# Three plain MLP steps ahead of 41 Strassen steps, with the token forms made behind six weight pieces

## The reference, cut to what matters

```python
h2 = rms_norm(x, norm2_g[layer]) * (1 + sc2[:, None]) + sh2[:, None]
ff = (jax.nn.silu(h2 @ w_gate[layer]) * (h2 @ w_up[layer])) @ w_down[layer]
x = x + g2[:, None] * ff
```

## Time and profile before

| | us |
|---|---|
| median of 3 runs | 2255.48 |
| lowest, highest | 2254.44, 2259.04 |
| the profiled execution | 2251.56 |
| its span | 2250.0 |

### The profile page before, as it was taken

How to read it: one execution, slowest core, us unless ns; L and a number is a source line. 1 busy time by engine, 2 the same in 40 slices (tenths; PEclk the granted TensorE clock), 3 DMA queues, 4 the chain that set the end, 5 groups by cost and what they waited for, 6 DMA issues and landing times.

```text
span 2250.0 us, 32144 instructions
## 1 busy us (share of the span) xinstructions
PE 2193.9 (98%) x10856; PEld 1831.2 (81%) x10856; DVE 1614.6 (72%) x2264; ACT 844.9 (38%) x1202; POOL 246.2 (11%) x300
## 2 busy tenths in 40 slices
PE   7999999999999998999999999999999999999996
PEld 4878888777777886888888888888888788888885
DVE  6986777777867898888988888889888522242234
ACT  4224333455453114444444444444444422232221
POOL 4012222000014331000000000000000000011111
PEclk9999999999999999999999999999999999999998
DMA  9895666533525982233333333333333633353333
GB/s 333 296 356 169 206 215 213 176 124 134 201 78 216 334 281 102 98 113 119 124 126 122 119 114 125 117 119 124 126 123 111 225 96 97 97 170 97 97 99 110
DMA packets 134552, 354.40 MB, mean 158 GB/s; under 512 B 21769, under 2 KB 46489, under 8 KB 133985
## 3 DMA queue, kind: packets, MB, share of 16 engines
q1 hardware_dynamic: 124498, 319.08, 42.6%
q0 software_dynamic: 8992, 34.41, 4.2%
q10 hardware_dynamic: 1008, 0.21, 0.0%
HBM read 334.47 MB, written 19.18 MB: 157 GB/s over the span
## 4 chain that ended last, share of the span: by engine, by line
PE 86%; DMA 5%; DVE 4%; POOL 2%; issue 2%; ACT 0%; SPq 0%; DVEq 0%; ACTq 0%; POOLq 0%
PE PS L930 10%; PE P L930 6%; PE PS L934 5%; PE T L983 4%; PE T L982 4%; PE T L981 4%; PE P L622 4%; PE P L624 3%; PE P L623 3%; PE P L934 3%; PE T L930 3%; PE S L930 3%; PE PS L622 3%; PE PS L623 3%; PE PS L624 3%; DMA adar<-in_w_ada 2%
## 5 line engine op out<-in xcount | busy, mean ns | idle before, releaser
L1439 DVE TENSOR_TENSOR W_lo<-raw,W_hi 128x1024 fp32r<-128x1024 f32 (+2 forms) x256 | 283.4, 1107 | 344.4 <-ACT W_hi L1012 343.7
L1012 ACT ACTIVATE W_hi<-raw 128x1024 fp32r<-128x1024 f32 (+2 forms) x256 | 236.8, 926 | 594.9 <-PE T L983 179.5
L1959 DVE TENSOR_TENSOR W_lo<-raw,W_hi 128x1024 fp32r<-128x1024 f32 x160 | 195.5, 1222 | 44.8 <-ACT W_hi L1328 40.7
L1328 ACT ACTIVATE W_hi<-raw 128x1024 fp32r<-128x1024 f32 x160 | 169.5, 1060 | 134.0 <-PE P L934 67.4
L1962 DVE TENSOR_TENSOR raw<-raw 128x1024 f32<-128x1024 f32 x160 | 194.7, 1217 | 0.0
L622 PE MATMUL PS<-H,W_hi 128*128 128x512 f32 x416 | 169.1, 406 | 18.3 <-POOL ident L2187 11.0
L622 PE MATMUL P<-H,W_hi 128*128 128x512 f32 x432 | 177.2, 410 | 4.0 <-DVE H L1915 3.3
L1328 ACT ACTIVATE H<-raw 128x1024 fp32r<-128x1024 f32 x120 | 126.8, 1057 | 133.3 <-DVE raw L1962 72.9
L624 PE MATMUL P<-H,W_lo 128*128 128x512 f32 x432 | 169.8, 393 | 0.0
L623 PE MATMUL P<-H,W_hi 128*128 128x512 f32 x432 | 169.7, 393 | 0.0
L624 PE MATMUL PS<-H,W_lo 128*128 128x512 f32 x416 | 164.0, 394 | 0.0
(11 more groups left out here) (334 smaller groups left out, 4854.7 us busy)
## 6 DMA issues: line engine op xcount, KB each, us to landing
raw<-in_w_gu SPq DMA_DIRECT2D x176, 512.0 KB, 3.3
raw<-in_w_in SPq DMA_DIRECT2D x72, 512.0 KB, 3.5
adar<-in_w_ada SPq DMA_DIRECT2D x72, 512.0 KB, 4.5
att<-in_w_ada SPq DMA_DIRECT2D x32, 1024.0 KB, 10.7
att<-in_w_ada SPq DMA_DIRECT2D x56, 512.0 KB, 5.1
raw<-in_w_down SPq DMA_DIRECT2D x64, 384.0 KB, 3.1
raw<-in_w_down SPq DMA_DIRECT2D x64, 320.0 KB, 2.8
raw<-in_w_out SPq DMA_DIRECT2D x32, 512.0 KB, 5.0
```

The lines of the kernel that those rows point to most:

```text
L1012: act.activation(w_parts(slot)[0][:, 0:cols], raw[:, raw_slot * PW:raw_slot * PW + cols], ACT.Copy).then_inc(hi_done, 1)
L1328: act.activation(form_parts(FORM_SLOT[a])[0], raw_form(FORM_RAW[a]), ACT.Copy).then_inc(hi_done, 1)
L1439: dve.tensor_tensor(lo[:, 0:cols], raw[:, raw_slot * PW:raw_slot * PW + cols], hi[:, 0:cols].bitcast(F32), ALU.subtract).then_inc(lo_done, 1)
L1959: dve.tensor_tensor(lo, raw_form(FORM_RAW[a]), hi.bitcast(F32), ALU.subtract).then_inc(lo_done, 1)
```

## The change

NPL falls from 4 to 3, so step 3 is made as a Strassen step, 41 in all, and all counters that start from NPL move with it. The parts of the T forms now have only two plain steps, 1 and 2, with six pieces: a table T_AT gives the parts behind each, (0), (1, 2), (3, 4), (5), (6), (7). The low parts of part 7 stand in the last plain step behind part 7 (and the low parts of 6). `make_t(u)` has a new wait, for all six instructions of the part before it, since it writes `Ea` and `Eb` again and two parts may now follow each other without a split between them.

```diff
-NPL = 4
+NPL = 3
+T_AT = ((0,), (1, 2), (3, 4), (5,), (6,), (7,))
 FS = FT - NPL
...
             for f in range(1, NPL):
                 for j in range(1, 4):
                     split_gu(f, j)
-                    if 3 * f - 4 + j < HALF:
-                        t_high_half(3 * f - 4 + j)
+                    for u in T_AT[3 * f - 4 + j]:
+                        t_high_half(u)
                 act.wait_ge(used, MLP0 + 4 * f + 2)
...
                 s0 = 6 * u
+                if u:
+                    dve.wait_ge(t_step, s0)
                 half = slice(u * HS, u * HS + HS)
...
             for f in range(1, NPL):
                 for j in range(1, 4):
                     split_gu(f, j)
-                    u = 3 * f - 4 + j
-                    if u < HALF:
+                    for u in T_AT[3 * f - 4 + j]:
                         make_t(u)
-                    if 0 < u <= HALF:
-                        t_low(u - 1)
+                        if u > 0:
+                            t_low(u - 1)
+                if f == NPL - 1:
+                    t_low(HALF - 1)
                 split_gu(f + 1, 0) if f < NPL - 1 else split_form(NPL, "A11")
```

## The result

The changed kernel takes 2264.17 us (median of 5 runs, 2261.30 to 2265.91) against 2255.48 us before (5 runs, 2252.93 to 2259.04): ratio 1.0038, 95% interval 1.0027 to 1.0049. It is slower by 0.38%, 8.6 us, between 6.1 and 11.0.

The account below looks back on a forecast made before the run. The prediction took TensorE, busy 98% of the span, to bound the kernel. It summed -2.20 + 5.67 + 1.6 = +5.1 us onto the median 2255.48, giving 2260.6 us, 0.22% slower, range 2257.0 to 2264.5.

Parts of the forecast that it names:

- The step saved: In the MLP, a plain step of 21.76 us on TensorE becomes a Strassen step of 19.56 us: -2.20 us.
- The chain of splits: Pieces 2 and 3 of step 1: two T parts behind one split delay the next weight pieces on TensorE, +5.67 us.
- Step 2 and the switch: Step 2 and the passage to form A11: one part per piece, split done 1.8 us ahead of need, nothing lost.
- The clock: Behind TensorE's 4.1 us idle: one stretch at 1.2 GHz, +1.6 us, from a price between 0 and 3.2.
- The three rows that I compared: Earlier TensorE pauses bounding the clock price: 2.02 and 2.19 us brought a fall to 1.2 GHz, 2.88 us did not.
- The third rival: TensorE's pauses bring a further slow clock stretch: +1.6 us more, 2262.2 us, or 2263.8 with both; chance 0.19.
- The second rival: ScalarE's and VectorE's queues overlap, hiding the doubled parts: no wait over 2.2 us in sum, 2253.3 with none; chance 0.06.

Follow-up runs that it names:

- the repeat: The changed kernel measured once more with no edit: 2265.20 us against 2255.95 before, ratio 1.0034.
- the evenly placed parts: Changed kernel, parts 0 and 1 behind piece 1, then one behind each split, ScalarE copying weight pieces ahead of T copies: 2254.44 us against 2255.95 before.
- ScalarE's order: Changed kernel, with only ScalarE copying a weight piece ahead of the second part's T copies, VectorE's order kept: 2259.82 us, ratio 1.0022 to before.
- doubled parts alone: Changed kernel with four plain steps again, keeping only the new placing of the T parts and the new wait: 2266.55 us, ratio 1.0042 to before.
- one doubled piece: Changed kernel with four plain steps, only parts 1 and 2 behind one split, all others single: 2257.89 us, ratio 1.0009 to before.
- the one with the busy pause: Changed kernel plus twelve unused matmuls on TensorE ahead of piece 0 of step 2: 2259.89 us, ratio 1.0017 to before.

## Why the prediction was right, point by point

The direction, the two late pieces and what they wait for were forecast as they came. The number is 3.5 us short of the measured 8.6, and it was in part luck that the median fell inside the range, by 0.3 us: the repeat's 2265.20 us lies above it. Here is each term.

**The step saved, -2.20 us: right.** 802.83 - 783.27 = 19.56 us for the added Strassen step, and the evenly placed parts, with no wait left, gave the 2.20 us back in the profile.

**The chain of splits, +5.67 us: right, term by term.** Piece 3 of step 1 was forecast 1.2 us late and is 1.09 late (920.44 - 902.91 against 916.52 - 900.08); the idle of TensorE is 0.93 us where some 1.0 was said. Piece 0 of step 2 was forecast 5.56 us late and is 5.46 late, with 4.08 us of idle for 4.1 forecast. Step 2 and the switch bring no wait, as said. The added wait cost nothing that shows: part 2, which it guards, starts 1.35 us after the low halves ahead of it (913.63 and 914.98 us), where the rows gave 1.34.

**The clock, +1.6 us: the term that was mis-sized.** The mechanism was right, since with TensorE kept busy 2.95 us came back. But behind the pause of 4.08 us the clock stayed at 1.2 GHz not for some 3.4 us as behind the pauses of 2.02 and 2.19 us but for 6.1, and 15 matmuls took 6.41 us for 3.41: with the restart that is 3.03 us in the changed kernel, 2.64 in its repeat, and 1.53 behind the 3.40 us pause of the run with ScalarE's order changed. I took a price from pauses half as long. The three rows that I compared are of one execution, and how long the clock stays down moved the sum, not only the spread. The row nearest to this pause in length, 2.88 us without a fall, spoke for less, and was one outcome of two: the pause at that place brought a fall in 4 of the 8 profiles that left it as it was.

**The sum.** -2.20 us, 5.46 us of lateness and the 3.03 us with restart and clock make +6.3 us, what the stretch shows, and 2261.8 us. The median lies 2.4 us above that. The third rival, more clock than one stretch, gives 2262.2 to 2263.8 us and is nearest. Its mechanism came in part: the first pause brought no fall, the second brought one nearly twice as long, and the pause ahead of the down projection brought one in the profile of the changed kernel and in its repeat. The second rival, waits hidden by overlap of the queues, is excluded for this order, and right for another one: its argument for, that VectorE has the time in steps 1 and 2, is what the even placing used.

**What stays open.** In seven comparisons the difference to before, by the ratio, lies above what the stretch shows, by 0.4 to 2.3 us: +8.6 for +6.3, +7.7 for +5.9, +9.5 for +8.4, +3.8 for +3.5, +5.0 for +3.9, +2.0 for +1.6, -1.6 for -2.2. Each difference is inside its interval, but all have one sign. The granted clock of every run, not only of the profiled ones, points at falls of the clock elsewhere. Its mean is 0.9872 in the changed kernel and in its repeat, and 0.9896 in the 27 runs of before. Counted as (1 - clock) x span, an estimate that takes TensorE as always busy, the changed kernel lost 5.5 us more than before, give or take 2, where the stretch has 3.0 and 2.6. In the same count the other kernels lost more than their stretch shows too, by 1.8 (doubled parts alone), 2.0 (ScalarE's order), 1.4 (one doubled piece) and 1.0 us (evenly placed), and the one with the busy pause 0.4 less. That is the size of what is open, but each figure is uncertain by 1 to 2 us, and no run shows which pauses it is or why they would cost more with the change.

## What to carry to other kernels

When work on one engine has to fit behind pieces that another engine consumes at a fixed pace, sum the work over each piece and not over the stage: here it fitted in total (42.5 of 43.6 us) and still cost 8.4 us where two pieces in a row carried 9.2 us of it against a pace of 5.44 and a lead of 2.86. Put the split that is waited for ahead of work that is not, on each engine that handles it. And count a pause of the matmul engine together with the matmuls behind it: filling four pauses with matmuls whose result is dropped took the kernel with evenly placed parts from 1.6 to 6.5 us below before, more than the 2.2 us that the change had to give. Most of that gain is not the change's: these pauses are in the kernel before as well, and filling them there was not run.

## What the runs showed of the hardware

The clock's fall depends on more than the length of one pause: 2.02 and 2.19 us brought it in the profile of before and 2.88 us didn't, and ahead of the down projection pauses of 3.15, 2.76, 2.73 and 2.62 us brought it where 2.88, 2.66, 2.60 and 2.56 us did not. Behind the same pause of 4.08 us the matmuls ran at 1.2 GHz for 6.1 us in two profiles and for 5.3 in a third, and behind one of 3.40 us for some 2.9. Matmuls whose result nobody reads held 2.4 GHz at all five places where they were put in, and 1.44 us of idle left behind twelve of them brought no fall. The kernel with the filled pauses also spread less, seven times between 2247.51 and 2250.53 us where 29 times of the kernel before on the same chip lie between 2250.84 and 2260.82; its mean granted clock is 0.993 against 0.990. That the filled pauses are the reason for the smaller spread was not tested.
